# Block inverses of both scan directions joined by one set of matmuls, two sample tiles at a time

## The reference

```
mod = silu(cond) @ w_ada[layer] + b_ada[layer]        # shift, scale, gate rows
p = h @ w_in ; q, k = l2norm(silu(dwconv3(p))) ; v = silu(dwconv3(p))
m = where(strict, (k*beta) @ k.T * decay, 0)          # per chunk and head
a = m + I
u = solve(a, v*beta) ; w = solve(a, k*beta*exp(gc))   # unit lower triangular
v_new = u - w @ s
o = (q*exp(gc)) @ s + attn @ v_new
s = s*g_last + (k*exp(gc_last - gc)).T @ v_new
# the same again on the flipped sequence: the backward direction
y = concat(rmsnorm(o_f + flip(o_b)) * silu(gate), short_conv) @ w_out
```

## Time and profile before

| | |
|---|---|
| median of three runs | 1465.14 us |
| profiled execution, first to last instruction (span) | 1463.3 us |
| TensorE matmul busy | 1398.1 us, 96% |
| VectorE busy | 980.4 us, 67% |
| ScalarE busy | 414.9 us, 28% |
| GpSimd busy | 502.4 us, 34% |
| mean granted TensorE clock | 0.985 |

### The profile page before, as it was taken

How to read it: one execution, slowest core, us unless ns; L and a number is a source line. 1 busy time by engine, 2 the same in 40 slices (tenths; PEclk the granted TensorE clock), 3 DMA queues, 4 the chain that set the end, 5 groups by cost and what they waited for, 6 DMA issues and landing times.

```text
span 1463.3 us, 24324 instructions
## 1 busy us (share of the span) xinstructions
PE 1398.1 (96%) x9514; PEld 1364.2 (93%) x9514; DVE 980.4 (67%) x1458; ACT 414.9 (28%) x765; POOL 502.4 (34%) x302
## 2 busy tenths in 40 slices
PE   6999999899697999999999999999999999999997
PEld 4899899899696999999999999988999999999997
DVE  4864889776765778778788887487773255325554
ACT  4545243463514322012210322462110011001122
POOL 0000200005043333553356336114544455455650
PEclk9999999999899999999999999999999999999999
DMA  9633122531232335344345442112332224222202
GB/s 373 238 130 101 44 71 80 211 123 77 76 101 86 101 115 197 130 153 143 113 140 177 132 139 101 44 44 83 103 101 81 77 72 145 76 77 79 70 13 72
DMA packets 44716, 164.24 MB, mean 112 GB/s; under 512 B 4848, under 2 KB 7536, under 8 KB 42608
## 3 DMA queue, kind: packets, MB, share of 16 engines
q1 hardware_dynamic: 44656, 163.45, 32.3%
HBM read 155.04 MB, written 6.82 MB: 111 GB/s over the span
## 4 chain that ended last, share of the span: by engine, by line
PE 77%; DVE 8%; issue 8%; ACT 3%; POOL 2%; DMA 1%; ACTq 0%; SPq 0%; POOLq 0%; DVEq 0%
PE ps L821 60%; PE ps L1291 3%; PE ps L1168 3%; POOL wlo L713 2%; PE ps L1238 1%; PE ps L1198 1%; ACT work L1503 1%; PE ps L873 1%; PE ps L833 1%; PE ps L967 1%; DMA work<-in_zeros 1%; PE ps L1099 1%; PE ps L1097 1%; PE ps L1087 1%; PE ps L937 1%
## 5 line engine op out<-in xcount | busy, mean ns | idle before, releaser
L821 PE MATMUL ps<-hhi,whi 128*128 128x320 f32 x1904 | 439.0, 312 | 14.8 <-DVE hlo L1890 9.3
L821 PE MATMUL ps<-hhi,wlo 128*128 128x320 f32 x1904 | 435.1, 310 | 0.0
L821 PE MATMUL ps<-hlo,whi 128*128 128x320 f32 x1904 | 435.0, 310 | 0.0
L821 PEld LDWEIGHTS ps<-hhi,whi 128*128 128x128 f32 x1904 | 320.4, 189 | 20.2 <-issue 14.4
L821 PEld LDWEIGHTS ps<-hlo,whi 128*128 128x128 f32 x1904 | 320.2, 189 | 0.0
L821 PEld LDWEIGHTS ps<-hhi,wlo 128*128 128x128 f32 x1904 | 320.0, 189 | 0.0
L708 POOL TENSOR_TENSOR wlo<-raw,whi 128x1024 fp32r<-128x1024 f32 (+1 forms) x92 | 232.8, 2530 | 7.7
L705 POOL TENSOR_SCALAR whi<-raw 128x1024 fp32r<-128x1024 f32 (+1 forms) x92 | 96.7, 1052 | 357.5 <-PE ps L821 266.6
L713 POOL TENSOR_TENSOR wlo<-raw,whi 128x1024 fp32r<-128x1024 f32 x44 | 110.0, 2499 | 210.2 <-ACT whi L1771 210.2
L1778 ACT ACTIVATE work<-ps 128x640 f32<-128x640 f32 x44 | 31.1, 707 | 427.2 <-PE ps L821 425.3
L2459 DVE TENSOR_TENSOR hidlo<-work,hidhi 128x640 fp32r<-128x640 f32 (+1 forms) x44 | 105.0, 2386 | 41.2 <-ACT hidhi L1788 41.2
(11 more groups left out here) (273 smaller groups left out, 1806.1 us busy)
## 6 DMA issues: line engine op xcount, KB each, us to landing
raw<-in_w_gu SPq DMA_DIRECT2D x88, 512.0 KB, 3.2
ada_raw<-in_w_rows SPq DMA_DIRECT2D x70, 512.0 KB, 3.5
raw<-in_w_in SPq DMA_DIRECT2D x28, 512.0 KB, 3.3
raw<-in_w_dn SPq DMA_DIRECT2D x24, 448.0 KB, 3.3
ada_first<-in_w_ada SPq DMA_DIRECT2D x8, 1024.0 KB, 18.2
raw<-in_w_dn SPq DMA_DIRECT2D x16, 512.0 KB, 3.4
row_late<-in_w_rows SPq DMA_DIRECT2D x10, 512.0 KB, 3.4
raw<-in_w_out SPq DMA_DIRECT2D x8, 512.0 KB, 4.5
```

Source lines behind the costliest of these rows:

```text
L821: last = nc.tensor.matmul(pair[pr][:, b], wt[:, cs], act[:, k, b * HALF:(b + 1) * HALF], start=(j == 0 and q == 0), stop=(j == len(tiles) ...
```

## The change

The two directions of a tile now go through one set of joins. The forward matrix is zero on one side of the diagonal and the backward matrix on the other, so `combine` (ScalarE) copies the backward blocks into the empty half of the forward slot, one `y` matmul serves both, and the `z` products are placed into forward and backward slots by small copies of single blocks instead of 128x512 additions. `place` spreads the small inverses: for the prompt on ScalarE, for the four sample tiles at once (16 matrices in one instruction) on VectorE, ScalarE and GpSimd. The prompt tile's `y5`, `z5`, `y6` stand between the gate units 25, 26 and 27; the sample tiles follow in two rounds of two tiles (`for l in (1, 3)`). GpSimd clears the spare blocks. `rinv` is laid out by direction first.

The ten row sums of the join rounds are gone from there: six more are done in the input stage, four more in the output stage. The clearing of `flat` is split into two transfers, the first of them behind the load of unit 23.

```diff
-ROWS_IN, ROWS_B = [0, 1, 1, 1, 1, 0, 1, 0], [1, 2, 2]
-ROWS_LOAD = {5: 1, 6: 1, 7: 1, 8: 1, 10: 1, 13: 1, 14: 1, 15: 1}
-ROWS_JOIN, ROWS_OUT = 10, [1, 1, 1, 1, 0, 0, 0, 0]
+ROWS_IN, ROWS_B = [0, 1, 1, 1, 1, 2, 1, 1], [2, 1, 3, 2]
+ROWS_LOAD = {5: 1, 6: 1, 7: 1, 8: 1, 9: 2, 10: 1, 11: 1, 12: 2, 13: 1, 14: 3}
+ROWS_OUT = [1] * KD
-PAIRS = [(NT - 1, 0), (NT - 1, 1)] + [(s if c == 0 else NT - 2 - s, c) for s in range(NT - 1) for c in range(2)]
+JOIN = [NT - 1, *range(NT - 1)]
+TTX_OF, RDX_OF, TT2_OF, R5_OF = (0, 1, 0, 1), (1, 0, 1, 0), (0, 0, 1, 1), (1, 1, 0, 0)
...
+                elif u == U_V + 3:
+                    sp.wait_ge(s_am, 2 * NT)
+                    sp.wait_ge(s_conv, PRIMED + NQK + NB)
+                    sp.dma_start(flat[:, 2560:4608], t["zeros"][:, 0:2048]).then_inc(s_clear_r, 16)
-            sp.wait_ge(s_am, 2 * NT)
-            sp.dma_start(flat[:, 0:4096], t["zeros"]).then_inc(s_clear_r, 16)
-            sp.wait_ge(s_ex, 2)
+            sp.dma_start(flat[:, 0:2560], t["zeros"][:, 0:2560]).then_inc(s_clear_r, 16)
+            sp.wait_ge(s_pex, 3)
...
-            sp.dma_start(cond_late[:], t["cond_save"]).then_inc(s_cond_rows, 16)
-            for _ in range(2):
-                load_rows(rows)
-                rows += 1
-            while rows < ROWS_LATE:
-                load_rows(rows)
-                rows += 1
-            sp.wait_ge(s_ex, 2 * NT)
+            sp.wait_ge(s_tt2, NT - 1)
+            sp.wait_ge(s_r5, NT)
             sp.dma_start(x[:, 0:3], t["x_save"][:, 0:3]).then_inc(s_back[0], 16)
-            sp.wait_ge(s_rinv, 2 * NT)
+            sp.wait_ge(s_fin, NT)
+            sp.wait_ge(s_pex, 5)
...
+            pool.wait_ge(s_attn_work, 48)
+            nc.gpsimd.memset(flat[:, 4608:6144], 0.0).then_inc(s_tz, 1)
+            pool.wait_ge(s_y6, 1)
+            for i, (rows, columns) in enumerate(((blk(1), blk(0)), (blk(2), blk(3)))):
+                pool.wait_ge(s_tz, 1 + i)
+                nc.gpsimd.memset(tt2_p[rows, :, columns], 0.0).then_inc(s_tz, 1)
+            clear_backward(NT - 1, 1, 3)
+            pool.wait_ge(s_blk, 2)
+            src, _ = inverted("R", 1, 1)
+            for q in range(Q):
+                pool.wait_ge(s_tz, 6 + q)
+                nc.gpsimd.tensor_copy(rinv_m[blk(q), NT * NH:(2 * NT - 1) * NH, blk(q)],
+                                      matrices(src, blk(q), NH * (NT - 1))).then_inc(s_tz, 1)
+            for l in (2, 4):
+                pool.wait_ge(s_y6, l + 1)
+                clear_backward(l - 2, 2, 7 + 3 * l // 2)
+            pool.wait_ge(s_tz, 16)
             pool.wait_ge(s_tok, 2 * NT)
             for s in range(NT):
                 for c in range(2):
...
+            def y5(l):
+
+                n, buf = JOIN[l], join_bufs(l)[0]
+                if l == 0:
+                    pe.wait_ge(s_pex, 2)
+                    pe.wait_ge(s_dx, 2 * NT)
+                    pe.wait_ge(s_mt, 2 * NT)
+                    pe.wait_ge(s_am, 2 * NT)
+                else:
+                    pe.wait_ge(s_fin, 1)
+                if l >= 3:
+                    pe.wait_ge(s_y6a, l - 1)
+                    pe.wait_ge(s_y6d, l - 2)
+                for h in range(NH):
+                    last = nc.tensor.matmul(bank[y_bank(l)][:, h], rinv[:, n, h], buf[:, h], start=True, stop=True)
+                last.then_inc(s_y5, 1)
+
+            def z5(l):
+
+                buf = join_bufs(l)[1]
+                pe.wait_ge(s_y5a, l + 1)
+                if l:
+                    pe.wait_ge(s_y5d, l)
+                    pe.wait_ge(s_pex, 6)
+                if l >= 3:
+                    pe.wait_ge(s_fin, l - 1)
+                    pe.wait_ge(s_zt1, l - 1)
+                for h in range(NH):
+                    last = nc.tensor.matmul(bank[z_bank(l)][:, h], buf[:, h], ys5[:, ys(l), h], start=True, stop=True)
+                last.then_inc(s_z5, 1)
+                for h in range(NH):
+                    last = nc.tensor.matmul(bank[zt_bank(l)][:, h], ys5[:, ys(l), h], buf[:, h], start=True, stop=True)
+                last.then_inc(s_z5, 1)
+
+            def y6(l):
+
+                n, buf = JOIN[l], join_bufs(l)[2]
+                if l == 0:
+                    pe.wait_ge(s_pex, 4)
+                else:
+                    pe.wait_ge(s_tt2, l)
+                for h in range(NH):
+                    last = nc.tensor.matmul(bank[y_bank(l)][:, h], rinv[:, n, h], buf[:, h], start=True, stop=True)
...
+                if u > U_G:
+                    (y5, z5, y6)[u - U_G - 1](0)
-            for l in range(0, 2 * NT, 2):
-                y5(l)
-                y5(l + 1)
-                tokens(l // 2, 0)
-                z5(l)
-                z5(l + 1)
-                y6(l)
-                y6(l + 1)
-                tokens(l // 2, 1)
-                z6(l)
-                z6(l + 1)
+            pe.wait_ge(s_r5, 1)
+            tokens(0, 1)
+            z6(0)
+            pe.wait_ge(s_zt1, 1)
+            tokens(0, 0)
+            for i in range(1, 3):
+                for j in (1, 0):
+                    tokens(i, j)
+            for l in (1, 3):
+                for step, filler in ((y5, ()), (z5, ((3, 1),) if l == 1 else ((4, 1),)),
+                                     (y6, ((3, 0),) if l == 1 else ((4, 0),)), (z6, ())):
+                    step(l)
+                    step(l + 1)
+                    for i, j in filler:
+                        tokens(i, j)
...
+            def combine():
+
+                act.wait_ge(s_mt, 2 * NT)
+                for rows, columns in BACKWARD:
+                    last = nc.scalar.activation(rinv_m[rows, 0:NT * NH, columns],
+                                                rinv_m[rows, NT * NH:2 * NT * NH, columns], ACT.Copy)
+                last.then_inc(s_pex, 1)
+
+            def place(dst, kind, of, l, n):
+
+                for q in range(Q):
+                    last = nc.scalar.activation(dst[blk(q), :, blk(q)],
+                                                matrices(inverted(kind, of[q], l)[0], blk(q), n), ACT.Copy)
+                return last
...
+            act.wait_ge(s_blk, 1)
+            act.wait_ge(s_clear_r, 16)
+            place(ttx_p, "T", TTX_OF, 0, NH)
+            place(rdx_p, "R", RDX_OF, 0, NH)
+            for c in range(2):
+                last = place(rinv[:, c * NT + NT - 1], "R", (c,) * Q, 0, NH)
+            last.then_inc(s_pex, 1)
             gate(0)
             weight_hi(U_G + 2)
-            expand_pair(0)
+            place(tt2_p, "T", TT2_OF, 0, NH)
+            place(r5_p, "R", R5_OF, 0, NH).then_inc(s_pex, 1)
             gate(1)
             weight_hi(U_G + 3)
-            expand_pair(1)
+            act.wait_ge(s_y5, 1)
+            act.wait_ge(s_clear_y5, 16)
+            y5_blocks(0, ((1, 0), (3, 2), (0, 1), (2, 3)))
             gate(2)
+            act.wait_ge(s_z5, 1)
+            for f, g in ((1, 0), (2, 3)):
+                last = nc.scalar.activation(tt2_p[blk(f), :, blk(g)], bank[z_bank(0)][blk(f), :, blk(g)], ACT.Copy)
+            last.then_inc(s_pex, 1)
+            r5_blocks(0)
             gate(3)
-                if l + 2 < 2 * NT:
-                    expand_pair(l + 2)
-                y6_copy(l)
-                y6_copy(l + 1)
-                token_copy(l // 2, 1)
-                if l + 2 < 2 * NT:
-                    expand_pair(l + 3)
+            act.wait_ge(s_blk, 2)
+            act.wait_ge(s_clear_r, 32)
+            act.wait_ge(s_tz, 3)
+            place(flat[:, 2048:4096].rearrange("p (m e) -> p m e", e=P), "R", RDX_OF, 1, NH * (NT - 1)).then_inc(s_pex, 1)
+            for l in (1, 3):
+                if l == 3:
+                    act.wait_ge(s_z6, l)
+                place(flat[:, 5120:6144].rearrange("p (m e) -> p m e", e=P), "R", R5_OF, l, 2 * NH)
+                for ll in (l, l + 1):
+                    act.wait_ge(s_y5, ll + 1)
+                    act.wait_ge(s_z5, 2 * (ll - 1))
+                    y5_blocks(ll, ((1, 0), (3, 2)))
+                for ll in (l, l + 1):
+                    r5_blocks(ll)
+                token_copy(l // 2 + 3, 1)
+                for ll in (l, l + 1):
+                    act.wait_ge(s_y6, ll + 1)
+                    act.wait_ge(s_z6, ll - 1)
+                    y6_block(ll, 2).then_inc(s_y6a, 1)
+                for ll in (l, l + 1):
+                    joined(ll, 1, BACKWARD[:2]).then_inc(s_zt1, 1)
+                token_copy(l // 2 + 3, 0)
...
+            some_rows(ROWS_B[0])
             body_conv(0)
             weight_lo(11)
-            some_rows(ROWS_B[0])
+            some_rows(ROWS_B[1])
             body_gate(0)
             weight_lo(12)
-            some_rows(ROWS_B[1])
+            some_rows(ROWS_B[2])
             weight_lo(13)
+            some_rows(ROWS_B[3])
             body_conv(1)
             weight_lo(14)
-            some_rows(ROWS_B[2])
...
+            dve.wait_ge(s_pex, 3)
             lanes_out(d_blk)
-            for l in range(0, 2 * NT, 2):
```

(76 more changed lines are left out.)

211 lines of the change are left out of this document (95 added, 116 removed).

## The result

| | before | after |
|---|---|---|
| median (4 runs each) | 1465.89 us | 1446.53 us |
| profiled execution, span | 1463.3 us | 1445.4 us |
| TensorE matmul busy | 1398.1 us | 1377.6 us |
| mean granted clock | 0.985 | 0.982 |

The ratio is 0.9866 with a 95% interval of 0.9852 to 0.9880. The forecast was 1442.8, in a range of 1435 to 1452: the change is faster, 19.4 us by the medians where 22.3 were forecast.

The account below looks back on a forecast made before the run. TensorE, busy nearly all the launch, was taken as the bound, with joins bound by matmuls and their number of rounds. Terms -4.2 + 0.3 - 19.5 - 0.4 + 1.5 = -22.3 took 1465.1 to 1442.8 us, range 1435 to 1452.

Parts of the forecast that it names:

- part 3: Joins: placing 5.2 us, then two rounds of 10.9, 2.5 for the clock; scan starts earlier, -19.5 us, ends -17 and -24.
- part 5: Output stage: weights queue behind row tiles' loads that wait for row sums; +1.5 us, bounds 0 and 4.
- rival C: Output stage gated in full, every one of the last units and the hand-over: 1.5 becomes 4 or 5, 1446; chance 12%.
- Part 1: Input stage: row sums ahead of the scaling remove 2.54 us of wait and 1.66 of half clock; -4.2, bounds 2.5 and 4.2.
- Part 2: End of the input stage: `combine` delays the rounding for unit 22 by about 0.3 us; prompt placing is absorbed; +0.3.
- Rival B: Joins: small copies are dear, 1 us each beside two other engines, placing 8.0; +5, 1448 us; chance 15%.
- Part 4: Start of the scan: a row sum of 1.22 us behind the last join is gone; -0.4, bounds 0 and 1.2.
- Rival A: The input stage's gain of 4.2 us is lost to later waits and not there at the end: 1447; chance 20%.
- Rival D: TensorE stays at half clock through joins, 17 us more, 1460; with scan steps 1467 to 1495; chance 5%, one step or more.
- Rival E: Joins: a buffer or bank wait makes a round's two tiles go one after the other, 16 us a round: 1453; chance 3%.

Follow-up runs that it names:

- the fillers: The changed kernel with 20 fp32 matmuls of 128x128 without use in TensorE's idle time ahead of the first sample join; 1444.37 us (1443.07 to 1446.40).

## Why the prediction was right, and where a size was off

The time lies in the stated range, and part 3, nearly the whole of the gain, came by the mechanism named: two rounds in place of four. One part failed. The prediction called itself wrong if the output stage lost more than 4 us, and in this trace it lost 5.97, outside part 5's bounds of 0 and 4. The total hides this, since part 3 gained 1.25 more than forecast and the range was wide. By the total alone the 1446 of rival C fits better than the 1442.8; only the stages show that one unit of the output stage was hit and not each.

- Part 1 (-4.2): right in this pair of traces, to 0.01. But what was read as one price is two: 2.55 of wait, which came back when undone, and 1.66 of half clock, which two other executions with the same wait do not show (the rows put back, and the short sums in the kernel before). Its lower bound, 2.5, is as likely as its value.
- Part 2 (+0.3): +0.25.
- Part 3 (-19.5): -20.75. Of the working's terms, placing was 4.7 (5.2 taken, the upper end), the clock 1.3 (2.5, the upper end of the 1.3 to 2.5 that six traces show), and the rest, from the first `y5` to the scan less that 1.3, 22.7 (21.8 and 0.4). A wait of 1.20 for the `ys` blocks in round 2 and one of 1.29 ahead of the scan are in it. Rival B, 1 us a copy, falls; its cause was real at a smaller size (0.73 against 0.42).
- Part 4 (-0.4): -0.25.
- Part 5 (+1.5): +5.97, and this is where the forecast lost its 3 us. The mechanism was the one named, a row tile's load waiting ahead of the weights, and rival C had its price ("1.5 becomes 4 or 5"), though not its extent: one of the last units waits, not every one. The terms: one new wait of 2.93 where 1 to 2.4 a unit were reckoned; 1.63 of half clock behind it, which the working left out although part 1 had just used it; 0.5 at the first unit, whose two executions differ only in when the clock rose (a cause seen in the traces, not tested); and 0.88 at the end, which the working left out: VectorE's last row sum stands ahead of the norm there, and half of it took 3.29 beside GpSimd (with the last four sums short TensorE's idle time there is 6.63 again). The new wait is in every trace with this queue order, 2.77 to 2.93 where the fourth sum is whole, but not its half clock: the stage took 88.87, 88.61 and 88.36 in the traces of the changed kernel, of the fillers and of the rows put back, and 87.11 with GpSimd's copies late, where the clock stayed at 1.00. So part 5 costs 4.2 to 6.0 by the execution. The cycle was reckoned with a turn of 6.6 to 7.0 from the earlier trace rows; here it was 8.0 (406.27 to 414.27), since the sum ran beside GpSimd.
- Rival A: fell, by two experiments. Rival D: the clock was at 1.00 in 3.5 us. Rival E: each round has its two tiles in step.
- Two figures of the working do not follow from its own terms: part 3's low end is -25, not -24 (3.5 + 0.4 + 20.6 = 24.5 us against 49.5), and A, B and C together give 1455 to 1456, not 1457. Neither bears on the forecast.

What stays open is why a wait of 2.5 to 2.9 us drops the clock in some executions (3.44 for the Gram products in the kernel before; behind 2.93, 2.89, 2.84 and 2.82 in the output stage) and not in others (2.05 for the Gram products behind 2.55; behind 2.77 in the output stage). No run was made on that.

## What to carry to other kernels

Merging chains pays where a profile shows rounds with a fixed period of dependent matmuls. Work that stands beside such rounds is nearly free there: the row sums gave 0.5 us by leaving, and the queue order that four of them brought into the output stage cost 4 to 6. Each load that waits for a late event holds every load behind it in the queue: before moving work, ask what its transfer is queued in front of, and put it one place later. And a wait of TensorE costs more than its length, since the clock may fall with it.

## What the runs showed of the hardware

- A VectorE operation of 64 columns with two SBUF inputs took 2.42 us beside a GpSimd subtraction, 0.21 alone; a copy of 32x512 took 0.73 beside a GpSimd copy and 0.42 alone, with ScalarE's copies beside it either way.
- Behind 3.7 to 5.1 us of idle time TensorE was at half clock in all six traces, and this cost 1.3 to 2.5 us (the same matmuls took 6.80 to 8.02, and 5.52 behind fillers). Behind waits of 2.54 and 2.55 ahead of the Gram products the clock fell in one execution and not in two.
- The start of the launch differs by up to 2.55 us between executions (43.41 to 45.96 at the marker), ahead of every edit.
